# Averages of three heads by column groups in quarters, spread by transfers, with DVE's slots laid out anew and layer one's weight sums on POOL

## The chip, the cores and the metric

One core of a Trainium2 chip runs the whole program. The engines are PE (TensorE, matrix products), DVE (VectorE), ACT (ScalarE), POOL (GpSimd) and SP (SyncE, which here issues most transfers). The metric is the device time of one execution in microseconds (us); lower is better.

## The reference, cut to what matters

The program is one inference step of a two-layer decoder. Layer one (layer A) has an mLSTM branch with four heads of 256 channels and an attention branch over a memory; layer two (layer B) attends over windows. A prompt of 1024 tokens and eight single samples go through it together, so W = 1032 columns (1024 + 8) stand side by side. The change touches the end of the mLSTM branch:

```
(C1, n1, m1), hs = lax.scan(_mlstm_chunk_step, ...)
h = sigmoid(o_pre) * hs                          # per head, 256 channels
mu = mean(h, axis=-1)                            # over the head's 256 channels
var = mean(square(h - mu), axis=-1)
hn = (h - mu) * rsqrt(var + EPS) * g_hn
y = hn + skip * xc
y_mix = y * silu(zg)
```

Here `o_pre`, `zg` and others come from the product `z = rmsnorm(x) @ w_in_a`, which runs while the heads are finished.

## The kernel before

Channels lie on partitions and tokens in columns: a head is two tiles of 128 x 1032 (`big(6 * h)` and `big(6 * h + 1)`), and two more (`HELD[h]`) are its scratch.

**Products.** All projections are made by a scheme with seven smaller products in the place of eight (Strassen's, Winograd's form). A *slot* is one such product: four f32 matmuls of 128 x 258 on PE (L3206, eight records in the trace, since each f32 matmul makes two). A *unit* is seven slots, and two units share one *pair* of weight tiles, so a pair lasts 14 slots. In layer A the loop variable x counts the slots, 0 to 153. Slot x runs product j = x % 7 of its unit. DVE adds five of the seven products into the unit's tiles, a slot later and from PSUM: U2 after j = 1 (L3392), U3 after j = 3 (L3394), C22 (L3397), C21 (L3400) and C12 (L3403). PE waits for them: j = 3 for U2, j = 0 for the previous unit's U3, j = 1 for its C21, j = 4 for its C12, j = 6 for C22. U2 and C22 are the tight ones: the sum can start when slot 1 (5) of the unit ends, and PE wants it one slot later, at the start of slot 3 (6).

**Weights.** SP loads a pair of weight tiles (1 MB, `RING<-in_w_in_a`) at the start of each 14 slots. The scheme wants sums of the tiles. In layer A, DVE makes them in slots 10 and 11 of each 14 (`sum_pair_dve`, L2800 to L2809, five instructions of up to 128 x 512); in layer B, POOL does (`sum_pair`, L2780 to L2788, in instructions of 128 x 256, 384 and 128).

**Heads.** `GATE = (7, 35, 63, 91)` says at which slot x each head begins; n = x - GATE[h]. DVE (`head_dve`, L1484 on): n = 0, 1 small sample operations (L1476 to L1479) and the gates (L1494, two of 128 x 1032); n = 6 the sum of the head's two tiles (L1497, "values sum"); n = 10, 11 centre (L1502, minus the mean, which it reads in PSUM); n = 14 the sum of the squares (L1507); n = 20, 21 norm (L1512); n = 22, 24 skip (L1519); n = 25, 27 the multiplication with zg (L1528; for head 3 at slots 129 and 131). The averages over a head's channels are PE's: `average` (L1341) multiplies the summed tile with a 128 x 128 matrix of 1/256, so each row of the result holds the same averages for all columns. They stand at MEAN = GATE + 8 and VAR = GATE + 16, behind the first matmul of that slot. ACT squares (GATE + 12), takes the logarithm from PSUM (`root_log`, GATE + 17) and the exponential (`root_exp`, GATE + 18) into `ROOT`, a 128 x 1032 tile. SP loads the skip tiles `xc` of heads 2 and 3 at GATE of two heads before + 26.

**State pairs.** The samples' 32 states (8 samples, 4 heads) are updated one after the other by `states_at`, at x % 7 = 2 and 5: SP loads, POOL multiplies (L1200, two of 128 x 256), ACT reduces and decays (L1215, L1208), DVE adds (L1230, two), SP stores. Two buffers take turns, XTRA and TRIG (every fourth is TRIG). The last of them is made near slot 86.

Each engine runs its instructions in the order in which the program writes them, and waits on semaphores. Nothing is moved by a scheduler: a stalled instruction holds all behind it on its engine.

## Time and profile before

| what | us |
| --- | --- |
| median of 3 runs | 1780.26 |
| lowest and highest | 1778.36 and 1782.37 |
| the profiled execution | 1782.37 |
| its span, first to last instruction | 1780.5 |

The profiled execution is the slowest of the three, 2.1 us above the median; 1.9 us of it lie outside the span. The profile has for each engine its busy time, groups of instructions with their mean duration, a chain of waits followed back from the end, and rows in order of time. In these a row joins a few like instructions, "[idle before <-releaser]" tells how long the engine had stood and who let it go on, and a PE row is longer than its slot by the matmul's tail, so that slots are read from the starts. PE is a matmul, PEld the load of its weights.

### The profile page before, as it was taken

Reading aid. Unit: us, or ns where it says so; the run is one execution under the profiler, and the core shown is the slowest. Engines: PE = TensorE matmul, PEld = TensorE weight load, DVE = VectorE, ACT = ScalarE, POOL = GpSimd, SP = SyncE. Lnnn points to the kernel's source line nnn. Section 1 sums busy time; section 2 is a strip of 40 time slices with the busy share of each in tenths; the row PEclk is TensorE's granted clock in tenths of the full one; section 3 lists DMA queues with packets and bytes.
Section 4 is the critical chain, followed back from the end, with each engine's and each line's share of the span. In section 5 each row is a group of like instructions: output and inputs, shape, how many; then the busy total and the mean of one; then the engine's idle time right before and its main releaser. Section 6 shows DMA issues by size and latency. Waiting matters only on the chain.

```text
span 1780.5 us, 22514 instructions
## 1 busy us (share of the span) xinstructions
PE 1754.5 (99%) x8318; PEld 1377.2 (77%) x8318; DVE 855.3 (48%) x1799; ACT 617.7 (35%) x1505; POOL 460.6 (26%) x511
## 2 busy tenths in 40 slices
PE   9999999999999999999999999999999999999998
PEld 5577765988888888747558888888888888779573
DVE  1444323785666556451342543354435444776613
ACT  1321234553655245211311133423242334843311
POOL 0151200335222012410003552154326443223000
PEclk9999999999999999999999999999999999999999
DMA  7312112145655245531111112223132434844422
GB/s 267 136 60 68 63 56 60 49 154 170 192 176 162 77 108 156 187 129 48 61 70 48 37 35 91 72 65 107 45 111 72 142 117 127 278 143 148 156 70 96
DMA packets 149078, 196.21 MB, mean 110 GB/s; under 512 B 19083, under 2 KB 108171, under 8 KB 148834
## 3 DMA queue, kind: packets, MB, share of 16 engines
q1 hardware_dynamic: 140708, 174.58, 30.7%
q10 hardware_dynamic: 8262, 20.20, 3.0%
q8 instruction: 66, 1.08, 0.2%
q14 instruction: 42, 0.34, 0.1%
HBM read 156.97 MB, written 37.85 MB: 109 GB/s over the span
## 4 chain that ended last, share of the span: by engine, by line
PE 90%; DVE 5%; ACT 2%; issue 1%; DMA 1%; SPq 0%; POOL 0%; ACTq 0%; DVEq 0%; POOLq 0%
PE PS L3206 49%; PE PS L2241 11%; PE PS L2285 4%; PE PS L2028 3%; PE PS L398 3%; PE PS L572 3%; PE PS L293 2%; PE PS L2064 2%; PE PS L2039 2%; PE PS L2061 1%; PE PS L934 1%; DVE WK L741 1%; PE PS L927 1%; PE PS L1348 1%; PE PS L2253 1%
## 5 line engine op out<-in xcount | busy, mean ns | idle before, releaser
L3206 PE MATMUL PS<-HT,RING 128*128 128x258 f32 (+2 forms) x1776 | 444.4, 382 | 2.7 <-ACT WK L3296 2.2
L3206 PEld LDWEIGHTS PS<-HT,RING 128*128 128x128 f32 x1776 | 329.6, 190 | 48.4 <-ACT WK L3296 3.1
L3296 ACT ACTIVATE BIG<-PS 128x256 f32<-128x256 f32 (+2 forms) x140 | 53.7, 383 | 354.1 <-PE PS L3206 353.6
L3206 PE MATMUL PS<-BIG,RING 128*128 128x258 f32 (+1 forms) x656 | 159.9, 382 | 1.3 <-DVE BIG L3392 1.3
L2241 PE MATMUL PS<-BIG 128*128 128x512 f32 x328 | 147.7, 597 | 0.5 <-DVE BIG L3403 0.5
L3206 PEld LDWEIGHTS PS<-BIG,RING 128*128 128x128 f32 x656 | 123.2, 190 | 19.6 <-DVE BIG L3392 2.1
L2241 PEld LDWEIGHTS PS<-BIG 128*128 128x128 f32 x328 | 60.4, 190 | 69.7 <-issue 68.6
L3206 PE MATMUL PS<-BIG,WK 128*128 128x258 f32 (+1 forms) x448 | 112.4, 382 | 1.0 <-DVE BIG L3392 1.0
L3206 PE MATMUL PS<-HT,CST 128*128 128x256 f32 (+2 forms) x432 | 110.3, 382 | 0.9 <-DVE BIG L3397 0.8
L3206 PEld LDWEIGHTS PS<-BIG,WK 128*128 128x128 f32 x448 | 83.4, 190 | 13.2 <-DVE BIG L3392 1.4
L3206 PEld LDWEIGHTS PS<-HT,CST 128*128 128x128 f32 x432 | 79.6, 190 | 12.5 <-DVE BIG L3397 2.1
L572 PE MATMUL PS<-WK,RING 128*128 128x344 f32 x288 | 84.3, 453 | 0.2 <-ACT BIG L652 0.2
L2080 ACT ACTIVATE WK<-WK 128x128 f32<-128x128 f32 (+1 forms) x96 | 42.4, 443 | 106.0 <-DVE WK L2112 106.0
L3394 DVE TENSOR_TENSOR BIG<-BIG,PS 128x256 f32<-128x256 f32 (+1 forms) x70 | 29.5, 422 | 99.3 <-PE PS L3206 99.2
L572 PEld LDWEIGHTS PS<-WK,RING 128*128 128x128 f32 x288 | 54.7, 190 | 28.7 <-ACT BIG L652 0.8
L2750 ACT ACTIVATE RING<-RING,VEC 128x256 f32<-128x256 f32 x176 | 74.7, 497 | 2.1 <-DMA RING<-in_w_kv_b 1.1
L3206 PE MATMUL PS<-WK,RING 128*128 128x256 f32 x288 | 73.5, 381 | 0.1
L3413 DVE TENSOR_TENSOR BIG<-BIG,TRIG 64x1024 f32<-64x1024 f32 (+1 forms) x48 | 67.6, 1408 | 1.2
L3067 POOL TENSOR_TENSOR BIG<-BIG 128x512 f32<-128x512 f32 x48 | 60.9, 1280 | 6.1 <-DVE BIG L3422 6.1
L3392 DVE TENSOR_TENSOR BIG<-BIG,PS 128x256 f32<-128x256 f32 (+1 forms) x70 | 29.5, 422 | 65.9 <-PE PS L3206 65.2
L3206 PEld LDWEIGHTS PS<-WK,RING 128*128 128x128 f32 x288 | 52.8, 191 | 7.1 <-DVE BIG L3392 0.7
L3400 DVE TENSOR_TENSOR BIG<-BIG,PS 128x256 f32<-128x256 f32 (+1 forms) x70 | 29.6, 423 | 57.8 <-PE PS L3206 57.6
(402 smaller groups left out, 3155.0 us busy)
## 6 DMA issues: line engine op xcount, KB each, us to landing
RING<-in_w_in_a SPq DMA_DIRECT2D x14, 1024.0 KB, 6.0
WK<-in_cache_mem_kv SPq DMA_DIRECT2D x56, 256.0 KB, 5.7
RING<-in_w_kv_b SPq DMA_DIRECT2D x12, 1024.0 KB, 5.6
RING<-in_w_in_b SPq DMA_DIRECT2D x12, 1024.0 KB, 5.3
WK<-in_cache_win SPq DMA_DIRECT2D x40, 256.0 KB, 4.6
RING<-in_w_mkv SPq DMA_DIRECT2D x16, 512.0 KB, 4.6
BIG<-in_x_prompt SPq DMA_DIRECT2D x16, 512.0 KB, 3.2
BIG<-sample_query SPq DMA_DIRECT2D x28, 256.0 KB, 5.8
```

Source lines behind the costliest of these rows:

```text
L293: last = nc.tensor.matmul(PS[:, s + b, 0:SEG], w[:, kt * P:(kt + 1) * P], rhs(kt, b * SEG, (b + 1) * SEG), start=(kt == 0), stop=(kt == kt ...
L398: last = nc.tensor.matmul(PS[:, 4 + 2 * nt + half, :], MEMT[:, kt, nt * P:(nt + 1) * P], w[:, half * 512:(half + 1) * 512], start=(kt == 0 ...
L572: last = nc.tensor.matmul(PS[:, s + b, 0:SEG], w[:, c:c + P], rhs, start=(kt == 0), stop=(kt == 1))
L2028: last = nc.tensor.matmul(bank[:, x * nk:(x + 1) * nk], q, k, start=True, stop=True)
L2080: last = nc.scalar.activation(p, PS[:, 3 + u % 2, x * nk:(x + 1) * nk] if g in MEM else p, ACT.Exp, bias=negmax[:, x:x + 1], scale=1.0 if ...
L2241: last = nc.tensor.matmul(PS[:, BANKS[i] + half, :], c.src(kt, u * P, (u + 1) * P), c.piece(kt)[:, half * 512:(half + 1) * 512], start=(kt ...
L2285: last = nc.tensor.matmul(PS[:, 6 + n % 2, 0:COLS], c.piece(kt)[:, n * P:(n + 1) * P], c.src(kt, 6 * P, W), start=(kt == 0), stop=(kt == c ...
L2750: last = nc.scalar.activation(x, x, ACT.Copy, scale=VEC[:, k, row:row + 1])
L3067: last = nc.gpsimd.tensor_tensor(perm(dst, d)[:, j0:j1], natural(big(RAW + x, 0, T), d)[:, j0:j1], natural(big(TURN + x, 0, T), d)[:, j0:j ...
L3206: last = nc.tensor.matmul(PS[:, bank, 0:mid - lo], weight_block(u // 2, s, k), h_block(layer_of(u), u % 2, t, k), start=(k == 0 and j not ...
L3296: nc.scalar.activation(part(u, n2 if j == 0 else n1, lo, mid), PS[:, banks(u)[0], 0:mid - lo], ACT.Copy).then_inc(sig("projections_copied" ...
L3413: last = nc.vector.tensor_tensor(y[q:q + 64], x[p:p + 64], TRIG[p:p + 64, W + lo:W + hi] .rearrange("p (t n) -> p t n", t=1).to_broadcast( ...
```

## The change

**Averages.** For heads 0 to 2 (`SPREAD = 3`) an average is four matmuls, each with 32 of the matrix's columns and a quarter of the tokens (258). They go to four groups of 32 rows in one PSUM bank, so that row group g holds quarter g. The mean stands at GATE + 4, the variance still at GATE + 16. Head 3 keeps the old form.

**Spread.** ACT brings the strip of 128 x 258 to `ROOT` (`mean_strip` at MEAN + 1, or logarithm at VAR + 1 and exponential at VAR + 2), and saves four rows of it, one of each group, to DRAM (`save_average`). At MEAN + 3 and VAR + 4 it waits for that and issues a transfer that reads the 1032 numbers back to all 128 rows of `ROOT` (`spread_average`, 516 KB written). DVE's centre and norm wait for it and read `ROOT`.

**DVE's slots for heads 0 to 2.** Gates 0, 1; values sum 3 (6 before); centre 10, 11; squares 14; norm 24, 25 (20, 21); skip 27, 32 (22, 24); zg 34, 35 (25, 27). For head 3: zg at 38, 40, as before; nothing else differs. Since the next head's gates stand at n = 28 and 29, norm, skip and zg of a head now surround these. The `xc` loads of heads 2 and 3 move from + 26 to + 33.

**Weight sums.** `sum_pair_dve` is gone; `sum_parts` on POOL makes layer A's sums too, in three parts at x % 14 = 5 (four instructions), 8 (two) and 9 (two), each behind what POOL has queued before.

```diff
-            job(f"mean{h}", "dve")
+            job(f"mean{h}", "act" if h < SPREAD else "dve")
...
-        MEAN = [x + 8 for x in GATE]
+        MEAN = [x + (4 if h < SPREAD else 8) for h, x in enumerate(GATE)]
         VAR = [x + 16 for x in GATE]
+        QUARTER = W // 4
...
-                    if x == GATE[h - 2] + 26:
+                    if x == GATE[h - 2] + 33:
...
         def layer_a_pool(pool):
+            parts = iter(())
             for x in range(XA):
                 for i in states_at(x + 2):
                     pair_pool(pool, i)
+                p = PF + x // 14 + 1
+                if x % 14 == 5 and p < PA:
+                    parts = sum_parts(pool, p)
+                if x % 14 in (5, 8, 9):
+                    next(parts, None)
...
-            for b in range(3):
-                last = nc.tensor.matmul(AVERAGED[:, b, :], avg_h, big(HELD[h][0], b * SEG, (b + 1) * SEG),
-                                        start=True, stop=True)
+            if h < SPREAD:
+                for g in range(4):
+                    last = nc.tensor.matmul(PS[32 * g:32 * (g + 1), 3, 0:QUARTER], avg_h[:, 0:32],
+                                            big(HELD[h][0], g * QUARTER, (g + 1) * QUARTER), start=True, stop=True)
...
+            act.dma_start(avg_rows_d[2 * h + var].rearrange("(g n) -> g n", g=4),
+                          ROOT[0:P:32, 0:QUARTER]).then_inc(average_saved(h, var)[0], 16)
...
+            act.wait_ge(*average_saved(h, var))
+            act.dma_start(ROOT, avg_rows_d[2 * h + var].partition_broadcast(P)).then_inc(average_spread(h, var)[0], 16)
...
+            nc.scalar.activation(ROOT[:, 0:QUARTER], PS[:, 3, 0:QUARTER], ACT.Copy).then_inc(job_read["act"].up(), 1)
+            save_average(act, h, 0)
...
+                        if x == MEAN[h] + 1:
+                            mean_strip(act, h)
+                        if x == MEAN[h] + 3:
+                            spread_average(act, h, 0)
+                        if x == VAR[h] + 4:
+                            spread_average(act, h, 1)
...
-            if n == 6:
+            if n == (3 if h < SPREAD else 6):
...
+            norm, skip, gated_at = ((24, 25), (27, 32), (34, 35)) if h < SPREAD else ((20, 21), (22, 24), (38, 40))
...
+                if h < SPREAD:
+                    dve.wait_ge(*average_spread(h, 0))
+                    ins = nc.vector.tensor_tensor(y, y, ROOT, ALU.subtract)
...
+                dve.wait_ge(*(average_spread(h, 1) if h < SPREAD else (sig("root_ready").sem, h + 2)))
...
-                if PF + x // 14 + 1 < PA and x % 14 in (10, 11):
-                    for n in ((0, 1), (2, 3))[x % 14 - 10]:
-                        sum_pair_dve(dve, PF + x // 14 + 1, n)
```

The order of instructions shows it. PE, head 0's mean in slots 14 and 15, before (a product is "x4" there):

```order
L3206 MATMUL PS<-HT,CST 128x258 x4
L3206 MATMUL PS<-HT,RING 128x258 x4
L3206 MATMUL PS<-BIG,WK 128x258
L1348 MATMUL PS<-BIG,CST 128x344 x3
L3206 MATMUL PS<-BIG,WK 128x258 x3
```

and after, in slots 11 and 12:

```order
L3252 MATMUL PS<-BIG,RING 128x258 x4
L3252 MATMUL PS<-HT,RING 128x258
L1358 MATMUL PS<-BIG,CST 32x258 x4
L3252 MATMUL PS<-HT,RING 128x258 x3
L3252 MATMUL PS<-BIG,RING 128x258 x4
```

The average is four matmuls of 32 x 258 where it was three of 128 x 344, and four slots earlier.

DVE, slots 62 to 67, where head 2's gates stand (L1230 is a state pair, TRIG or XTRA its buffer), before:

```order
L3400 TENSOR_TENSOR BIG<-BIG,PS 128x258
L1528 TENSOR_TENSOR BIG<-BIG 128x1032
L3403 TENSOR_TENSOR BIG<-BIG,PS 128x258
L1476 TENSOR_TENSOR SM<-SM 128x16
L1477 TENSOR_TENSOR SM<-SM 128x16
L1479 TENSOR_TENSOR BIG<-SM 128x2x8
L1494 TENSOR_TENSOR BIG<-BIG 128x1032 x2
L3392 TENSOR_TENSOR BIG<-BIG,PS 128x258
L1230 SCALAR_TENSOR_TENSOR XTRA<-XTRA,SM 128x256 x2
L2800 TENSOR_TENSOR WK<-RING 128x512
L2804 TENSOR_TENSOR RING<-RING 128x4x128
L3394 TENSOR_TENSOR BIG<-BIG,PS 128x258
```

and after:

```order
L3446 TENSOR_TENSOR BIG<-BIG,PS 128x258
L1581 SCALAR_TENSOR_TENSOR BIG<-WK,VEC,BIG 128x1032
L3449 TENSOR_TENSOR BIG<-BIG,PS 128x258
L1530 TENSOR_TENSOR SM<-SM 128x16
L1531 TENSOR_TENSOR SM<-SM 128x16
L1533 TENSOR_TENSOR BIG<-SM 128x2x8
L1548 TENSOR_TENSOR BIG<-BIG 128x1032 x2
L3438 TENSOR_TENSOR BIG<-BIG,PS 128x258
L1232 SCALAR_TENSOR_TENSOR XTRA<-XTRA,SM 128x256 x2
L1551 TENSOR_TENSOR BIG<-BIG 128x1032
L3440 TENSOR_TENSOR BIG<-BIG,PS 128x258
```

Head 1's skip (L1581) stands where its zg (L1528) stood, and head 2's values sum (L1551) where two of the weight sums stood.

POOL has state products and nothing else through layer A before (L1200). After, at the same stretch, it has:

```order
L1202 TENSOR_TENSOR WK<-TRIG 128x256 x2
L2845 TENSOR_TENSOR WK<-RING 128x256 x2
L2847 TENSOR_TENSOR RING<-RING 128x2x128 x2
L1202 TENSOR_TENSOR WK<-XTRA 128x256 x2
L2851 TENSOR_TENSOR WK<-RING 128x256 x2
L2854 TENSOR_TENSOR WK<-RING,WK 128x384
L2855 TENSOR_TENSOR WK<-RING,WK 128x128
L1202 TENSOR_TENSOR WK<-XTRA 128x256 x4
```

Eight weight sums stand among eight state products of 14 slots.

## Rows read from the trace of the kernel before

**Rows 1.** The page: busy times of the engines, granted clock of PE, chain of waits.

```profile
PE 1754.5 (99%) x8318; PEld 1377.2 (77%) x8318; DVE 855.3 (48%) x1799; ACT 617.7 (35%) x1505; POOL 460.6 (26%) x511
...
PEclk9999999999999999999999999999999999999999
...
PE 90%; DVE 5%; ACT 2%; issue 1%; DMA 1%; SPq 0%; POOL 0%; ACTq 0%; DVEq 0%; POOLq 0%
```

**Rows 2.** The averages' line: durations in ns (min/median/max), first and last start.

```profile
L1348 PE MATMUL PS<-BIG,CST x48: 452/453/453, 445.8 to 619.7; 128*128 128x344 f32 x48
```

**Rows 3.** PE's timeline at head 0's mean: start, us, engine, line, operation.

```profile
443.67 1.90 PE L3206 MATMUL PS<-HT,RING 128*128 128x258 f32 x8
445.41 0.60 PE L3206 MATMUL PS<-BIG,WK 128*128 128x258 f32 x2
445.84 1.90 PE L1348 MATMUL PS<-BIG,CST 128*128 128x344 f32 x6
447.58 1.47 PE L3206 MATMUL PS<-BIG,WK 128*128 128x258 f32 x6
448.88 1.90 PE L3206 MATMUL PS<-HT,RING 128*128 128x258 f32 x8
```

**Rows 4.** PE's timeline at the 32-column matmuls of L584.

```profile
259.68 3.93 PE L572 MATMUL PS<-WK,RING 128*128 128x344 f32 x13
263.54 10.62 PE L584 MATMUL PS<-BIG,TRIG 128*32 128x344 f32 x144
274.09 2.00 PE L293 MATMUL PS<-HT,RING 128*128 128x344 f32 x6
276.02 1.93 PE L594 MATMUL PS<-WK,TRIG 128*36 128x344 f32 x6
277.88 2.29 PE L293 MATMUL PS<-HT,RING 128*128 128x344 f32 x7
```

**Rows 5.** The weight loads of L584, timeline of PEld.

```profile
273.11 0.13 PEld L584 LDWEIGHTS PS<-BIG,TRIG 128*32 128x32 f32 x4 [0.16 <-issue]
273.40 0.13 PEld L584 LDWEIGHTS PS<-BIG,TRIG 128*32 128x32 f32 x4 [0.16 <-issue]
```

**Rows 6.** Timeline of DVE and POOL side by side, after layer A.

```profile
740.58 2.39 POOL L2780 TENSOR_TENSOR RING<-RING 128x256 f32<-128x256 f32 x2 [3.08 <-PE PS L3206]
...
740.81 6.57 DVE L2007 TENSOR_TENSOR BIG<-BIG 128x1024 f32<-128x1024 f32 x4
...
742.93 3.37 POOL L2782 TENSOR_TENSOR RING<-RING 128x256 f32<-128x256 f32 x2
```

**Rows 7.** Timeline of DVE and PE around head 2's gates.

```profile
536.48 0.36 DVE L1476 TENSOR_TENSOR SM<-SM 128x16 f32<-128x16 f32 x1
...
537.25 2.50 DVE L1494 TENSOR_TENSOR BIG<-BIG 128x1032 f32<-128x1032 f32 x2
...
539.67 0.42 DVE L3392 TENSOR_TENSOR BIG<-BIG,PS 128x258 f32<-128x258 f32 x1
540.00 0.88 DVE L1230 SCALAR_TENSOR_TENSOR XTRA<-XTRA,SM 128x256 f32<-128x256 f32 x2
...
541.16 1.91 PE L3206 MATMUL PS<-BIG,RING 128*128 128x258 f32 x8
```

**Rows 8.** POOL's state products: ns min/median/max.

```profile
L1200 POOL TENSOR_TENSOR WK<-XTRA x36: 722/740/1838, 421.5 to 569.0; 128x256 f32<-128x256 f32 x36
```

**Rows 9.** Transfers: size, median us to landing, issued from 321, 523 and 743.

```profile
WK<-mlstm_rows SPq DMA_DIRECT2D x1, 512.0 KB, 3.8
...
RING<-in_w_in_a SPq DMA_DIRECT2D x1, 1024.0 KB, 6.5
...
WK<-in_g_post ACTq DMA_DIRECT2D x1, 512.0 KB, 12.4
```

**Rows 10.** Timeline of POOL and DVE at head 0's TRIG state.

```profile
454.01 1.41 POOL L1200 TENSOR_TENSOR WK<-TRIG 128x256 f32<-128x256 f32 x2 [14.85 <-DMA TRIG<-sample_q_and_weighted_k]
...
457.42 0.41 DVE L3400 TENSOR_TENSOR BIG<-BIG,PS 128x258 f32<-128x258 f32 x1
```

More of the change, by code:

```diff
@@ L1346, in average, with average_saved, average_spread, save_average @@
                 pe.wait_ge(*read_of(f"mean{h}" if name[0] == "v" else f"var{h - 1}"))
-            for b in range(3):
-                last = nc.tensor.matmul(AVERAGED[:, b, :], avg_h, big(HELD[h][0], b * SEG, (b + 1) * SEG),
-                                        start=True, stop=True)
-            last.then_inc(job_done.up(), 1)
+            if h < SPREAD:
+                for g in range(4):
+                    last = nc.tensor.matmul(PS[32 * g:32 * (g + 1), 3, 0:QUARTER], avg_h[:, 0:32],
+                                            big(HELD[h][0], g * QUARTER, (g + 1) * QUARTER), start=True, stop=True)
+            else:
+                for b in range(3):
+                    last = nc.tensor.matmul(AVERAGED[:, b, :], avg_h, big(HELD[h][0], b * SEG, (b + 1) * SEG),
+                                            start=True, stop=True)
+            last.then_inc(job_done.up(), 1)
+        def average_saved(h, var):
+            return sig("scratch_saved").sem, 80 + 16 * (2 * h + var + 1)
+        def average_spread(h, var):
+            return sig("rows0_broadcast").sem, 16 * 3 + 16 * (2 * h + var + 1)
+        def save_average(act, h, var):
+            act.wait_ge(*(sig("root_ready").sem, h + 2) if var else read_of(f"mean{h}"))
+            act.dma_start(avg_rows_d[2 * h + var].rearrange("(g n) -> g n", g=4),
+                          ROOT[0:P:32, 0:QUARTER]).then_inc(average_saved(h, var)[0], 16)
+        def spread_average(act, h, var):
+            act.wait_ge(*average_saved(h, var))
+            act.dma_start(ROOT, avg_rows_d[2 * h + var].partition_broadcast(P)).then_inc(average_spread(h, var)[0], 16)
+        def mean_strip(act, h):
+            act.wait_ge(job_done.sem, done(f"mean{h}"))
+            if h > 0:
+                act.wait_ge(sig("y_ready").sem, 2 * h - 1)
+            nc.scalar.activation(ROOT[:, 0:QUARTER], PS[:, 3, 0:QUARTER], ACT.Copy).then_inc(job_read["act"].up(), 1)
+            save_average(act, h, 0)
         def woven_a_pe(pe, x):
@@ L1412, in root_log @@
             act.wait_ge(job_done.sem, done(f"var{h}"))
-            if h > 0:
+            if h < SPREAD:
+                nc.scalar.activation(ROOT[:, 0:QUARTER], PS[:, 3, 0:QUARTER], ACT.Ln,
+                                     bias=EPSC).then_inc(job_read["act"].up(), 1)
+            else:
                 act.wait_ge(sig("y_ready").sem, 2 * h - 1)
-            nc.scalar.activation(seg3(ROOT), AVERAGED, ACT.Ln, bias=EPSC).then_inc(job_read["act"].up(), 1)
+                nc.scalar.activation(seg3(ROOT), AVERAGED, ACT.Ln, bias=EPSC).then_inc(job_read["act"].up(), 1)
         def root_exp(act, h):
             act.wait_ge(*read_of(f"var{h}"))
-            nc.scalar.activation(ROOT, ROOT, ACT.Exp, scale=-0.5).then_inc(sig("root_ready").up(), 1)
+            root = ROOT[:, 0:QUARTER] if h < SPREAD else ROOT
+            nc.scalar.activation(root, root, ACT.Exp, scale=-0.5).then_inc(sig("root_ready").up(), 1)
+            if h < SPREAD:
+                save_average(act, h, 1)
         def gate_act(act, u):
@@ L1498, in head_dve @@
                                         ALU.add).then_inc(sig("values_summed").up(), 1)
[L1499 to L1502 removed]
+            centre, summed = 10, 14
+            norm, skip, gated_at = ((24, 25), (27, 32), (34, 35)) if h < SPREAD else ((20, 21), (22, 24), (38, 40))
+            if n in (centre, centre + 1):
+                e = n - centre
+                y = big(6 * h + e)
+                if h < SPREAD:
+                    dve.wait_ge(*average_spread(h, 0))
+                    ins = nc.vector.tensor_tensor(y, y, ROOT, ALU.subtract)
+                else:
+                    dve.wait_ge(job_done.sem, done(f"mean{h}"))
+                    ins = nc.vector.tensor_tensor(seg3(y), seg3(y), AVERAGED, ALU.subtract)
                 if e == 1:
[L1504 to L1505 removed]
+                    ins.then_inc((sig("values_summed") if h < SPREAD else job_read["dve"]).up(), 1)
+            if n == summed:
                 dve.wait_ge(sig("squares").sem, h + 1)
@@ L1508, in head_dve @@
                                         ALU.add).then_inc(sig("squares_summed").up(), 1)
-            if n in (20, 21):
-                y, j = big(6 * h + n - 20), 2 * h + n - 20
-                dve.wait_ge(sig("root_ready").sem, h + 2)
+            if n in norm:
+                e = norm.index(n)
+                y, j = big(6 * h + e), 2 * h + e
+                dve.wait_ge(*(average_spread(h, 1) if h < SPREAD else (sig("root_ready").sem, h + 2)))
                 nc.vector.scalar_tensor_tensor(out=y, in0=y, scalar=vec(ROW_GHN, j), in1=ROOT,
                                                op0=ALU.mult, op1=ALU.mult).then_inc(step.up(), 1)
-            if n in (22, 24):
-                e = (n - 22) // 2
+            if n in skip:
+                e = skip.index(n)
                 y, j = big(6 * h + e), 2 * h + e
@@ L2759, in sum_pair, with sum_parts @@
         def sum_pair(pool, p):
+            for _ in sum_parts(pool, p):
+                pass
+        def sum_parts(pool, p):
+            if p == PF + 1:
+                pool.wait_ge(sig("h_turned").sem, NU)
             if p < PA:
@@ L2783, in sum_pair @@
             then(last, 5)
+            yield
             for k in parts:
```

46 lines of the change are left out of this document (12 added, 34 removed).

## The prediction, before the kernel was run

> **What bounds the kernel now.** I read the page first. PE is busy for 99% of the span, at a granted clock of nine tenths or more in all forty slices, and the chain of waits that ended last lies for 90% on PE and for 5% on DVE [rows 1]. So what PE issues is the time, as long as nobody makes it wait. The reader should then look at the stretch where the averages stand. Their source line shows 48 matmul records of 453 ns, two per matmul, 24 matmuls in 8 averages [rows 2]. The PE timeline has no wait in brackets there, and shows that an average pushes the rest of its slot aside: the records of L1348 begin at 445.84 and the product goes on at 447.58, 1.74 us later; a slot without an average takes 443.67 to 445.41, also 1.74 us [rows 3]. One average is therefore worth a whole slot of PE, all of it on the path. In slots 0 to 111 every slot is 1.74 us but the eight with an average, at 3.47: PE waits for nobody there before the change, so each new wait shows in full.
>
> **What PE saves.** Six of the eight averages become four matmuls of 32 columns in four column groups. The trace has this form in L584: 144 matmuls of 32 columns, 344 wide [rows 4]; their weight loads come in fours, the fours 0.29 us apart (273.11 to 273.40) [rows 5]. That is the time of one full pass of 344 columns: the six records of L1348 take 1.74 us, 0.29 each [rows 3]. Four column groups thus share one pass. The new form is 258 wide; a slot has 8 passes of that width in 1.74 us, 0.217 each, and every f32 matmul makes two: 2 x 0.217 = 0.43 us. Going into that form and back costs something. In [rows 4] the 13 passes of L572 before it should end at 259.68 + 13 x 0.289 = 263.44 and L584 starts at 263.54 (0.11); its 36 passes should end at 273.94 and L293 starts at 274.09 (0.15). The 36-column form of L594 is dearer: 274.09 + 6 x 0.289 = 275.82 against 276.02 (0.20), and 276.02 + 6 x 0.289 = 277.75 against 277.88 (0.13). I take the dearer, 0.33, as the excursion is as short as that one. An average then costs 0.43 + 0.33 = 0.77 and saves 1.74 - 0.77 = 0.97; six save **5.8 us**. The bounds are 5.4 (switch 0.4) and 7.8 (no switch cost).
> The Trainium skill ("TensorE: Matmul & The Clock Gate", Measured speedup vs the span model) gives 2.38 times for three column tiles, 79% of the ideal; by it each pass of four would be 0.275 us and the six averages 0.7 us dearer, an estimate from that page, while L584 shows the whole factor.
>
> **What is moved beside PE.** ACT now copies or roots 258 columns instead of 1032, shorter than before. It adds two issues per average, on ACT's own queue; ACT is busy 35% of the span and delays nobody by them. DVE loses in ten weight pairs the five sums of L2800 to L2809, and POOL gets them: eight instructions for each pair. The last pairs' slots (121, 135) have waits for ACT and DVE today; the sums' going gives back perhaps 0.2 there, and as much may be lost, so nothing is entered. DVE's centre operations read SBUF instead of PSUM, for the same 1.2 us.
>
> **What POOL's sums cost DVE.** The trace shows what happens when POOL adds in SBUF while DVE runs operations with two SBUF operands. From 740.81 four DVE operations on 1024 columns take 6.57 us, 1.64 each, while POOL's take 1.19 and 1.69 [rows 6]; a lone DVE operation of 1032 takes 1.25 (2.50 for two) [rows 7], and a lone POOL one 0.72, with a maximum of 1.84 [rows 8]. DVE loses about 0.44 us for every POOL instruction that falls beside such work. Sums that read PSUM are never stretched (0.42 everywhere).
> The place where this matters is where a head's gates stand, since the two large multiplications are just ahead of a sum that PE needs. Head 2: before, smalls from 536.48, gates from 537.25, then the U2 sum, which ends at 540.09; PE takes its result at 541.16 [rows 7]. Slack 1.07. After, POOL has work all through it. The pair's load is issued at 523.9, lands after 6.5 us [rows 9], say at 531 with the spread beside it, and behind it stand eight sums and at least four state products at 1 to 1.2 us each: to about 543. The three smalls meet it (0.2 each is my estimate, between 0 and 0.4), and the two gates (0.44 each): 0.6 + 0.88 = 1.5. The work ahead (second norm from about 531, a pair of state operations, skip) is met by 1.2 more, of which I let only 0.1 pass: before the smalls stands a product sum that comes no earlier whatever DVE does. The U2 sum ends at 540.09 + 1.5 + 0.1 = 541.7, 0.5 after PE wants it.
> What is late next: the values sum now stands three slots behind the gates, after a pair of state operations (0.79) [rows 7]. From 541.65: 0.79 + 0.87 for two meetings, then 1.23 + 0.44, end 545.0. The average of slot 67 wants it one matmul into its slot: 541.16 + 1.74 = 542.9 [rows 7], + 0.5 + 0.43 = 543.8. PE waits another 1.15. **Head 2's window gives back 1.65.** Bounds: 0, if half of the meetings fall elsewhere, and 3.3 with twice the meetings.
> Head 1's window is built alike, with its norm a little later since its spread is: **1.8**. Head 3's has no state products left and its load lands earlier in it, and its values sum stays six slots behind the gates: 0 to 0.3, I take **0.1**.
>
> **The transfers.** Each new average is saved (4 rows of 258) and read back as a broadcast of 516 KB. The nearest rows are 3.8 us for a broadcast of 512 KB alone, 6.5 for 1 MB while others run, and 12.4 us for one of 512 KB issued by ACT into loaded queues [rows 9]. I take 4 to 5.5: around head 1 to 3 the queues carry one weight pair and small state loads. The mean's spread has two us to spare. The variance's is issued 0.8 us ahead of slot 56 (up to 2 us after slot 28), and DVE's norm can take it up to 6.6 us after its issue before the sums behind it are late. Nothing is entered; the upper end is a rival.
> Head 0 has another chain at that place. SP's loads into TRIG are released by the head's work; now PE's average stands four slots earlier, so what was loaded in slot 22's run-up comes 0.77 later against PE, and slot 22 starts 0.97 earlier. Before, POOL waits for that load at 454.01, and the C21 sum behind the TRIG pair ends at 457.83; slot 22 wants it at 448.88 + 6 x 1.74 = 459.3 [rows 3, 10]. Slack 1.5 less 1.74 leaves -0.24, and the spread shares the engines: **0.35** (0 to 1.5).
>
> **Sum.** Saved 5.8; given back 1.65 + 1.8 + 0.1 + 0.35 = 3.9. Net 1.9. The profiled execution has 1782.37 us, 2.1 above the median; so 1780.5 for a profiled run like it, and 1780.3 - 1.9 = **1778.4** against the median.
>
> **Rivals.**
> *The meetings are absorbed.* POOL's sums start early, or DVE's operations are stretched by less where POOL's are spaced by its waits; PE never waits. For it: the windows have 1.07 us of slack and the state products of POOL are spaced today (median 0.74, hardly stretched) [rows 8]. Against it: twelve or more instructions in a row and DVE busy from 531 on. Then 1780.3 - 5.8 + 0.35 = 1774.8; without a switch cost 1772.8.
> *The spreads land late: slower.* One mechanism: the 516 KB broadcast shares sixteen engines with the weight pair that SP issues within 2 us of it, and takes as long as the loaded one of [rows 9]. It decides from 6.6 us after the issue: DVE stands at the norm, and the sums of products queue behind it, and PE behind them. At 9 us the wait is 2.4 us for each of three heads: 7.2 more, 1785.5. Against it: 1 MB lands in 6.5 us in this very place.
> *DVE pays a whole POOL instruction.* Were each meeting to cost DVE all of POOL's 0.72 instead of 0.44, then some ten meetings in two windows cost 0.28 more each, some 2.2 a window on both: 1782.8. The row speaks against it (1.64, not 1.96) [rows 6].
> The Trainium skill ("SBUF — State Buffer", SBUF: two separate sides) states just this: an exclusive lock for the whole instruction between GpSimd and a DVE operation with two SBUF inputs, "the other fully blocks". The contention the trace agrees with, its full size not.
> *The column groups don't run side by side.* Eight passes of 0.217 and 0.33: 2.07 for an average against 1.74, 2 us lost where 5.8 should be won, and the windows' loss on top: 1786. L584's fours speak against it.
>
> **How the numbers follow.** Forecast 0.46; absorbed 0.34; late spreads 0.12; whole blocking 0.05; no packing 0.03. The measurement tells 0.2%, 3.6 us, from no change: below 1776.7 is faster, above 1783.8 slower. Faster takes the absorbed case and a tail of the forecast less a tail of the absorbed: 0.36. Slower takes the late spreads and no packing, less a little: 0.14. Same: 0.50. The range goes from the absorbed case with half the switch cost, 1773.8, to just short of the late spreads, 1784.0. The forecast's own range is 1775.5 to 1781.
>
> **What the new profile would show.** L1358's averages with 0.7 to 0.8 us between the product records around them; if 1.7, the packing fell. DVE's gates at 1.3 to 1.7 instead of 1.25 in heads 1 and 2, with PE idle in the slots that follow (three and four slots behind the gates' slot), released by DVE; if PE has no such idle time, my collisions were too dear and the time is near 1775. DVE idle before the norm or centre, released by a DMA into ROOT, would speak for the late spreads. The forecast fails most easily on the size and place of the meetings, as POOL's queue is ordered by waits and not by slots.

## The result: slower, and where the profile shows it

The changed kernel takes 1789.82 us (median of 6 runs, 1788.1 to 1793.12) against 1780.99 for the kernel before in the same comparison: a ratio of 1.0048, 95% interval 1.0038 to 1.0057. That is 8.8 us more, where the prediction had 1.9 less. The second rival of the prediction, spreads that land late, is what happened, and it cost more than the rival was given.

The page of the changed kernel, the lines that answer to [rows 1]:

```profile
span 1788.7 us, 22585 instructions
...
PE 1753.2 (98%) x8330; PEld 1369.5 (77%) x8330; DVE 836.9 (47%) x1749; ACT 615.6 (34%) x1508; POOL 533.7 (30%) x591
...
PE   9999999999899999999999999999999999999998
...
PE 81%; DVE 6%; issue 4%; ACT 4%; POOL 2%; DMA 2%; SPq 0%; ACTq 0%; DVEq 0%; POOLq 0%
```

PE is busy 1.3 us less and the span is 8.2 us longer: PE now waits. POOL has 73 us more work. PE's share of the chain of waits falls by 9 points, which go to issue, ACT, POOL, DVE and DMA. One slice of PE's row in layer A shows an 8 (the very last slice had its 8 before the change too).

The saving is there, as forecast. L1358, the average's line now (answers to [rows 2]), and the PE timeline at head 0's mean (answers to [rows 3]):

```profile
L1358 PE MATMUL PS<-BIG,CST x48: 381/393/406, 436.0 to 575.3; 128*32 128x258 f32 x48
```

```profile
435.48 0.60 PE L3252 MATMUL PS<-HT,RING 128*128 128x258 f32 x2
436.00 0.64 PE L1358 MATMUL PS<-BIG,CST 128*32 128x258 f32 x8
436.58 1.57 PE L3252 MATMUL PS<-HT,RING 128*128 128x258 f32 x6
437.99 1.91 PE L3252 MATMUL PS<-BIG,RING 128*128 128x258 f32 x8
```

That slot lasts 437.99 - 435.48 = 2.51 us where one without an average lasts 1.74: 0.77 for an average that cost 1.73.

The rest is in what PE waited for. In layer A's stretch (415 to 610) the kernel before has one wait of PE on the view, 1.6 us, ahead of the products. The changed kernel has these (engine, line, releaser: us in all, times, longest), and below them DVE's waits for the spreads, at the centre (L1560) and at the norm (L1574):

```profile
PE PS L3252 <- DVE BIG L3443: 8.6, 3, 3.9
PE PS L1358 <- DVE BIG L1551: 1.3, 2, 0.7
PE PS L3252 <- DVE BIG L3446: 0.9, 1, 0.9
PE PS L3252 <- DVE BIG L3438: 0.8, 1, 0.8
```

```profile
DVE BIG L1560 <- DMA WK<-head_averages: 9.3, 2, 5.4
...
DVE BIG L1574 <- DMA WK<-head_averages: 7.8, 2, 5.8
```

The largest sits in slot 33. The timeline of DVE there, then of PE:

```profile
471.79 0.87 DVE L1232 SCALAR_TENSOR_TENSOR XTRA<-XTRA,SM 128x256 f32<-128x256 f32 x2
478.50 1.67 DVE L1574 SCALAR_TENSOR_TENSOR BIG<-BIG,VEC,WK 128x1032 f32<-128x1032 f32 x1 [5.84 <-DMA WK<-head_averages]
480.09 0.41 DVE L3440 TENSOR_TENSOR BIG<-BIG,PS 128x258 f32<-128x258 f32 x1
480.43 1.42 DVE L1574 SCALAR_TENSOR_TENSOR BIG<-BIG,VEC,WK 128x1032 f32<-128x1032 f32 x1
481.77 0.41 DVE L3443 TENSOR_TENSOR BIG<-BIG,PS 128x258 f32<-128x258 f32 x1
```

```profile
476.47 1.91 PE L3252 MATMUL PS<-BIG,RING 128*128 128x258 f32 x8
482.23 3.55 PE L3252 MATMUL PS<-HT,CST 128*128 128x258 f32 x8 [3.86 <-DVE BIG L3443]
485.57 2.09 PE L3252 MATMUL PS<-HT,RING 128*128 128x258 f32 x8
```

DVE stands 5.84 us at the norm, since head 0's variance is not back. Two sums of products queue behind the two norms, and PE stands behind the second sum. When PE goes on, its slot takes 3.34 us, not 1.74. The same stretch by windows (us, PE busy, granted clock, share of the transfer engines, GB/s) says why:

```profile
470.00:476.50 6.50, 6.50 (x32) 1.00 0.85 278
476.50:482.20 5.70, 1.88 (x9) 1.00 0.34 121
482.20:485.60 3.40, 3.37 (x9) 0.55 0.32 89
485.60:489.00 3.40, 3.40 (x16) 0.95 0.41 143
```

After 3.86 us of PE's idleness the granted clock falls to 0.55, about the 1.2 GHz level, for 3.4 us, and then comes back to 2.4 GHz.

Slot by slot (from the starts of PE's products), slots 0 to 111 of layer A take 209.81 us before and 221.16 after, 11.35 more:

| slots | what | us |
| --- | --- | --- |
| 11, 15, 23, 39, 43, 51, 67, 71, 79 | six averages (slots 15, 43 and 71 lose their average, 11, 39 and 67 get it) | -5.78 |
| 33 to 35 | variance of head 0 late, the clock's fall 1.8 of it | +5.81 |
| 47, 48 | mean of head 1 late | +2.04 |
| 75 to 77 | mean of head 2 late, the clock's fall 1.8 of it | +4.89 |
| 21, 22 | head 0's TRIG state | +1.14 |
| 37 to 39 | head 1's gates and values sum | +1.08 |
| 65 to 67 | head 2's gates and values sum | +1.78 |
| 93, 94 | head 3's gates | +0.40 |

So the spreads' own slots cost 12.7 us, and the places that the prediction had priced cost 4.4 where it had 3.9.

The profiled execution reached slot 0 3.0 us earlier than the one before, in work that the change doesn't touch; hence 8.2 in the span and 11.4 in layer A. The timed runs put the change at 8.8.

### The profile page after: what moved, and what is told of

Same layout as the page of the kernel before. It is cut to its first block, busy times and chain, and to the rows that moved or that the text cites. A ratio compares the mean times of both kernels' runs of the same rounds, so it can differ in the third digit from the quotient of the medians.

```text
span 1788.7 us, 22585 instructions
## 1 busy us (share of the span) xinstructions
PE 1753.2 (98%) x8330; PEld 1369.5 (77%) x8330; DVE 836.9 (47%) x1749; ACT 615.6 (34%) x1508; POOL 533.7 (30%) x591
## 4 chain that ended last, share of the span: by engine, by line
PE 81%; DVE 6%; issue 4%; ACT 4%; POOL 2%; DMA 2%; SPq 0%; ACTq 0%; DVEq 0%; POOLq 0%
PE PS L3252 42%; PE PS L2299 11%; PE PS L2343 4%; PE PS L400 3%; PE PS L2086 3%; PE PS L574 3%; PE PS L295 2%; PE PS L2122 2%; PE PS L2097 2%; PE PS L2119 1%; DVE WK L743 1%; PE PS L936 1%; DMA WK<-head_averages 1%; PE PS L929 1%; POOL WK L1202 1%
## 5 line engine op out<-in xcount | busy, mean ns | idle before, releaser
L574 PEld LDWEIGHTS PS<-WK,RING 128*128 128x128 f32 x288 | 54.6, 190 | 28.7 <-ACT BIG L654 0.6
L3440 DVE TENSOR_TENSOR BIG<-BIG,PS 128x256 f32<-128x256 f32 (+1 forms) x70 | 29.5, 421 | 93.1 <-PE PS L3252 93.1
L2847 POOL TENSOR_TENSOR RING<-RING 128x256 f32<-128x256 f32 x76 | 68.8, 926 | 0.0
L2845 POOL TENSOR_TENSOR WK<-RING 128x256 f32<-128x256 f32 x34 | 28.1, 849 | 130.5 <-ACT RING L2808 86.1
L2845 POOL TENSOR_TENSOR RING<-RING 128x256 f32<-128x256 f32 x36 | 29.9, 852 | 100.9 <-ACT RING L2808 66.2
```

Of the source, the lines that this page charges most:

```text
L574: last = nc.tensor.matmul(PS[:, s + b, 0:SEG], w[:, c:c + P], rhs, start=(kt == 0), stop=(kt == 1))
L2845: nc.gpsimd.tensor_tensor(s3[:, k], a11[:, k], a21[:, k], ALU.subtract)
L2847: last = nc.gpsimd.tensor_tensor(a21[:, k], a21[:, k], a22[:, k], ALU.add)
```

## Why the spreads were late

When each spread (516 KB) was issued and landed, beside the weight pair (1 MB) of its time:

| spread | issued | pair issued | spread took |
| --- | --- | --- | --- |
| mean 0 | 438.84 | 442.28 | 4.0 |
| variance 0 | 469.71 | 468.16 | 8.8 |
| mean 1 | 500.90 | 500.00 | 7.7 |
| variance 1 | 527.37 | 527.19 | 6.5 |
| mean 2 | 555.13 | 554.28 | 9.0 |
| variance 2 | 583.39 | 584.17 | 4.5 |

The two that are issued ahead of their pair land in 4.0 and 4.5 us, the four behind it in 6.5 to 9.0. The packets say it directly. Of mean 1's spread (issued at 500.90 on ACT's queue, q10), in the view of transfers from 501 to 503.8, and then from 503.8 to 508.6:

```profile
q1 hardware_dynamic: 681, 0.79, 93.9%
q10 hardware_dynamic: 1, 0.00, 2.0%
```

```profile
q1 hardware_dynamic: 948, 0.95, 65.2%
q10 hardware_dynamic: 143, 0.52, 33.3%
```

For almost 3 us SP's queue moved 0.79 MB and ACT's next to nothing; then the spread went through. Not all of this is the pair's doing. The two spreads that are issued ahead also need 1.0 us before their first row moves; the four behind a pair need 2.6 to 4.1. And SP's queue held two state loads of 256 KB as well, issued 2.7 and 2.2 us ahead of mean 1's spread. The Trainium skill ("DMA: Bandwidth & Descriptors", Queues, rings and completion order) says that each engine takes turns between the queues that have work, packet by packet. Here the later queue's transfer did not get its turns at once: until a tenth of a late spread's rows had moved, SP's queue had moved 0.6 to 1.1 MB in the four cases. The measurement decides for this kernel.

The spread is only the second of two transfers in a row. The save of 4 KB ahead of it stands behind other loads in the same way: it took 1.6 to 2.4 us for mean 0 and the three variances, but 4.4 for mean 1 and 3.4 for mean 2. These two are issued 0.5 and 1.6 us behind the two `xc` loads of 516 KB, which the change itself had moved into slots 40 and 68:

```profile
496.00 0.81 SPq L1283 DMA_DIRECT2D WK<-xc_scratch  x2
496.49 0.50 ACTq L1377 DMA_DIRECT2D head_averages<-WK  x1
```

A mean has less time than a variance: DVE stood at head 1's centre from 504.7, 8.2 us after that save was issued.

## The experiments

Layer A means slots 0 to 111 of the profiled execution, against 209.81 us; the ratio is that of timed runs to the kernel before on the same chip, with its 95% interval.

**The spread ahead of the pair.**

```diff
+                if x % 14 == 0 and x // 14 in (2, 3, 4, 5):
+                    spread_average(sp, (x // 14 - 1) // 2, (x // 14 - 1) % 2)
                 if x % 14 == 0 and p >= PF + 2:
                     load_pair(sp, p)
...
-                        if x == MEAN[h] + 3:
+                        if x == MEAN[h] + 3 and h == 0:
...
-                        if x == VAR[h] + 4:
+                        if x == VAR[h] + 4 and h == 2:
```

> The changed kernel, but the four spreads that stood behind a weight pair in the transfer engines (variance of heads 0 and 1, mean of heads 1 and 2) are issued by SP just ahead of that pair. Theory 'queue': a spread is late because its packets stand behind the pair's 1 MB; in the changed kernel it landed in 4.0 and 4.5 us when issued ahead and 6.5 to 9.0 us when issued behind. It then expects four landings of 4 to 5 us and the long slots 33, 34, 47, 48, 75 and 76 back at 1.74 us, 12.5 us less: about 1777.5. Rival 'bytes': the 516 KB share the engines with the pair whichever comes first, landings stay at 7 to 9 us, and the time stays within 2 us of 1790. Rival 'POOL': the long slots come mostly from POOL's sums beside DVE; landings fall but less than half of the 12.5 us comes back: about 1784.

Layer A +0.36 us, ratio 1.0001 (0.9991 to 1.0010). The spreads' line:

```profile
L1385 SPq DMA_DIRECT2D WK<-head_averages x4: 332/332/332, 471.6 to 551.0; - x4
...
DMA to landing us min/median/max: 4.1/5.3/6.4
```

It was 4.0/7.1/9.0. Slots 33 to 35 are 1.74 again, 47 and 48 have 0.42 left and 75 and 76 0.48: 11.8 of 12.7 us came back. The edit changes two things, the order and the queue (SP's for ACT's). That the order counts with the queue kept shows in the spreads that ACT issues, in all kernels here: 15 issued ahead of the pair of their time landed in 3.9 to 4.8 us, 18 behind it in 5.6 to 9.0. Variance 2, which is always ACT's, lies on both sides: 4.5 to 4.8 ahead (5 times), 5.6 to 6.3 behind (6 times). Issued by SP ahead of the pair they took 4.6 to 7.0, so what else is under way costs something there too (6.4 for mean 1 here). Theory 'queue' holds; a rival 'bytes', with landings of 7 to 9 us, does not.

In the timed runs 8.4 us came back by the two ratios, some 4 less than I had expected. Of these, 0.9 is what slots 47, 48, 75 and 76 keep, and 0.8 is new: slots 37 to 39 lose 2.14 for 1.08 and head 3 0.57 for 0.40, while 65 to 67 (1.51) and 21 and 22 (1.02) lose a little less than before. The rest is that the profiled execution of the changed kernel showed more than its timed runs, 11.4 against 8.8. It may be that one wait had covered others: while PE was held up in slots 33 to 35, POOL's queue went on and met less of what came behind. No run shows this by itself, but the second execution of the changed kernel, further below, fits it: 6.7 us lost in slots 33 to 35 and nothing in 37 to 39.

**No spread.** The two issues are left out, and DVE's waits go to the save.

> The changed kernel without its spreads: the averages are saved, but not read back to all rows, so centre and norm use what lies in the tile. DVE waits for the save alone. Theory 'queue' and theory 'bytes' expect the same: slots 33, 34, 47, 48, 75 and 76 at 1.74 us, 12.5 us less, about 1777; the windows after the gates (slots 37 to 39 and 65 to 67) keep their 1.3 and 1.8 us, and head 0's slot 21 keeps about 1 us. Rival 'POOL' expects long slots there still, 1784 or more.

Layer A -3.67, ratio 0.9979 (0.9970 to 0.9989). All six slots are at 1.74. Left are 0.32 (slots 21, 22), 0.93 (37 to 39) and 0.87 (65 to 67). The timed runs say the same. So in this order of DVE's and POOL's work the change wins 3.7 without any spread, not 5.8. Against this run the changed kernel's profile has 15.0 us more, of which 12.7 are the spreads' own slots; the other 2.3 lie in slots 21, 22, 37 to 39, 65 to 67, 93 and 94, and whether the spreads' traffic makes them is not shown. The rival 'POOL' is out: no long slot is left.

**POOL's sums alone.**

```diff
 # the kernel before, and
+                if x % 14 == 5 and p < PA:
+                    parts = sum_parts(pool, p)
+                if x % 14 in (5, 8, 9):
+                    next(parts, None)
...
-                if PF + x // 14 + 1 < PA and x % 14 in (10, 11):
-                    for n in ((0, 1), (2, 3))[x % 14 - 10]:
-                        sum_pair_dve(dve, PF + x // 14 + 1, n)
```

> The kernel before, with one part of the change alone: layer one's weight sums on POOL in the same three parts. Averages, transfers and DVE's slots as before. By my sum the meetings of POOL's sums with DVE cost about 1.5 us in each of the two windows after the gates of heads 1 and 2; the values sum stands six slots behind the gates here and so waits for nobody. Expected: 0.5 to 1 us in slot 37 and in slot 65, nothing in slots 39 and 67, about 1782. Rival 'POOL': the sums cost several us, 1786 or more. Rival 'free': no slot gets longer, 1780 to 1781.

Layer A +1.71, ratio 1.0007 (0.9998 to 1.0017). Slots 37 and 38 lose 0.76, 65 and 66 lose 0.96, all others nothing. DVE and POOL around head 2's gates in this kernel:

```profile
536.91 0.59 DVE L1485 TENSOR_TENSOR BIG<-SM 128x16 f32<-128x16 f32 x1
537.61 3.58 DVE L1500 TENSOR_TENSOR BIG<-BIG 128x1032 f32<-128x1032 f32 x2
541.12 0.41 DVE L3383 TENSOR_TENSOR BIG<-BIG,PS 128x258 f32<-128x258 f32 x1
```

```profile
536.72 1.45 POOL L2796 TENSOR_TENSOR WK<-RING 128x256 f32<-128x256 f32 x2
538.24 1.86 POOL L2799 TENSOR_TENSOR WK<-RING,WK 128x384 f32<-128x384 f32 x1
540.07 1.44 POOL L2800 TENSOR_TENSOR WK<-RING,WK 128x128 f32<-128x128 f32 x1
```

The two gates take 3.58 us where they took 2.50 [rows 7]: 1.64 for the one that meets one POOL instruction and 1.91 for the one that meets two, 0.40 and 0.34 for each, where the prediction had 0.44. Even the operation on 16 columns takes 0.59 where it took 0.17.

**POOL's later parts held until the values sum**, for each head's gates.

```diff
-                if x % 14 in (5, 8, 9):
+                held_by = x // 28 if x // 14 in (0, 2, 4, 6) else None
+                if x % 14 in (5, 10, 11) if held_by is not None else x % 14 in (5, 8, 9):
+                    if held_by is not None and x % 14 == 10:
+                        pool.wait_ge(sig("values_summed").sem, 2 * held_by + 1)
                     next(parts, None)
```

> As the kernel with the spreads first, and in the 14 slots of each head's gates POOL's second and third part (four instructions) wait for the head's values sum, so that they don't meet the gates. Theory: the windows of slots 37 to 39 and 65 to 67 give back 1.3 and 1.8 us by meetings; half of those are with the held parts. Expected 1.0 to 2.5 us less than with the spreads first: about 1776. Rival: the state products alone meet the gates as often, and nothing changes beyond 0.5 us; or the sums come too late for slot 1 of the next pair and PE waits there.

Layer A +5.46, ratio 1.0032 (1.0021 to 1.0042). A miss, by one place: head 3's values sum stands six slots behind its gates, so its parts came too late, and PE stood 5.1 us on L2860, POOL's last sum, with the clock's fall behind it (7.8 us in slots 97 to 99). Elsewhere it lost 2.7 us less than with the spread first, a little more than expected.

**The same for three heads** (`(0, 2, 4)`).

> As e4_sums_held, without the holding in head 3's slots, whose values sum stands six slots behind its gates. Theory: the 7.8 us that slots 97 to 99 lost in e4_sums_held came from that holding alone and go; head 3's slot 93 has its 0.4 us back. Against the kernel before: saved 5.8, given back 0.2 (slot 21), 1.7 (37 to 39), 1.1 (65 to 67), 0.4 (93), 0.2 (117): 2.2 us faster than before, about 1779.5 on this chip. Rival: the held sums are late in other pairs too once these stalls are gone, and it is at the time of before.

Layer A -1.61, ratio 0.9994 (0.9984 to 1.0005), which the timed runs can't tell from no change. The 7.8 us are gone; slot 37 lost 1.58 where the same code had lost 0.50 in the run before: what meets what differs from one execution to the next.

**The values sum ahead of the state pair, and then the second gate behind the U2 sum.**

```diff
+                for h in range(H):
+                    if x == GATE[h] + 2:
+                        head_gate_dve(dve, h, 1)      # only in the second kernel
+                        if h < SPREAD:
+                            values_sum_dve(dve, h)
                 for i in states_at(x):
                     pair_dve(dve, i)
```

> As e5_held_three_heads, with the values sum of heads 0 to 2 ahead of the state pair that stands behind the gates. Theory: the average in slot 39 waits for the pair in front of the values sum (1.7 to 2.1 us with its meetings and its wait for ACT). Without it slot 39 loses its 1.1 us of wait; slots 37 and 65 keep 0.5 and 1.0, since the U2 sum stands ahead of both. 1.1 us faster than e5_held_three_heads. Rival: the pair, now later, makes PE or the next state late, and the gain is under 0.3 us.

> As e6_values_sum_ahead, with the second gate of each head behind the U2 sum, which the first gate alone then stands ahead of. Theory: PE's waits in slots 37, 65 and 93 come from the U2 sum behind two stretched gates (1.65 us each); with one of them moved, they go: 0.5, 1.0 and 0.4 with 0.1 each for going on, 2.0 us less than e6_values_sum_ahead. The values sum is 0.4 us later and its average in slots 39 and 67 may wait up to 0.5 us. About 1776. Rival: the sum of the three operations is the limit and PE's wait moves whole to slots 39 and 67, no gain.

Layer A +1.06 and +2.89, ratios 0.9999 (0.9990 to 1.0009) and 1.0009 (0.9999 to 1.0018). In each the aimed-at wait went: slots 39 and 67 have no wait in the first, slots 37, 65 and 93 none in the second. Yet in the profiled executions both lost more in layer A than the kernel that they started from (-1.61); the timed intervals overlap, so the runs leave this open. Most of what was new is in slots 47, 48 and 75 to 77, which lost 2.6 and 5.7 us: the means' spreads went out late, in slots 43 and 71, then in 44 and 72 (42 and 70 in the kernel that they started from). I took SP's store of the later state pair for the cause, since it stands ahead of the spread in SP's queue, and the next experiment was built on that. The trace says otherwise. What SP waited for at mean 1's spread (L1388) in the second kernel is the save (SP's waits from 490 to 500):

```profile
SPq L1388 <- DMA head_averages<-WK: 2.1, 1, 2.1
```

The two means' saves took 5.4 and 6.1 us in the first kernel and 5.8 and 6.8 in the second, where they had taken 4.2 and 4.5; all of them are issued 0.5 us behind the two `xc` loads. Why they are slower here is not shown. Neither my theory nor the rival had this.

**The mean's spread on ACT again, and then the TRIG state's loads ahead of the pair of slot 14.**

```diff
-                if x % 14 == 0 and x // 14 in (2, 3, 4, 5):
+                if x % 14 == 0 and x // 14 in (2, 4):
...
+                if x == GATE[0] + 7:                  # only in the second kernel
+                    pair_load(sp, EARLY_STATES + 3)
                 if x % 14 == 0 and p >= PF + 2:
                     load_pair(sp, p)
...
-                        if x == MEAN[h] + 3 and h == 0:
+                        if x == MEAN[h] + 3:
```

> As e7_second_gate_later, but the means' spreads are issued by ACT again; SP still issues the variance's of heads 0 and 1 ahead of its pair. Theory: in e7_second_gate_later SP came to the mean's spread only in slots 44 and 72, since the state pair behind the values sum is later and SP's store of it stands ahead; so DVE's centre was late and slots 47, 48 and 75 to 77 lost 5.7 us. ACT can issue them at slot 42 and 70 + 1 us: 4 to 5 us less than e7_second_gate_later, about 1778. Rival: ACT's spread then shares with SP's two state loads and lands after 6 us or more; half of the loss stays.

> As e9_mean_by_act, and at slot 14 SP issues the loads of the TRIG state ahead of the weight pair instead of behind it. Theory: slot 21's wait (0.8 to 1.4 us in the kernels with spreads) is the TRIG state landing behind the pair's 1 MB at slot 20; ahead of it, it lands before slot 18 and the wait goes: 1 us less than e9_mean_by_act, 3 us less than the kernel before. Rival: slot 21 waits for something else, POOL's or ACT's work on that state, and the gain is under 0.3 us; or the pair, now behind, makes POOL's sums late.

Layer A +6.51 and +1.26, ratios 1.0026 (1.0014 to 1.0038) and 1.0010 (1.0001 to 1.0019). The first is a miss, since its theory had the wrong cause. ACT has to wait for the save just as SP had:

```profile
493.99 0.48 ACTq L1382 DMA_DIRECT2D head_averages<-WK  x1
499.73 0.34 ACTq L1388 DMA_DIRECT2D WK<-head_averages  x1
500.17 0.39 ACT L3358 ACTIVATE BIG<-PS 128x258 f32<-128x258 f32 x1 [4.74 <-DMA head_averages<-WK]
```

So ACT issued the spreads 2.3 and 1.5 us into slots 43 and 71, 2.2 and 2.1 us behind SP's pair, and they landed after 6.6 and 6.5 us, in slots 47 and 75. ACT's copies of products stood behind that wait too, and PE waited 1.3 and 0.5 us for them in slots 43 and 71.

The second removes slot 21's wait whole (1.35 us to 0), as expected, though this kernel too is not faster than the kernel before. How long before slot 22's turn the TRIG loads land goes with the loss in slots 21 and 22 in every kernel here: 5.4 us in the kernel before and 7.1 in this one, no loss; 4.4, 0.08 lost; 4.3, 0.23; 3.4, 1.14; 3.0, 1.46.

**The changed kernel again.**

> The changed kernel once more, for its stalls from execution to execution. Theory: each spread behind a pair lands late in each execution; slots 33, 47 and 75 are long again by 1.5 us or more each, 8 to 13 us in sum, and the clock falls only behind those waits that are over about 2 us. Rival: the profile first seen was one of the bad ones, and the sum here is under 8 us. The part ahead of layer A, which the change does not touch, should differ by up to 3 us either way.

Layer A +8.70, ratio 1.0044 (1.0028 to 1.0059). The spreads behind their pair took 8.1, 7.9, 6.8 and 7.5 us, those ahead 4.2 and 4.5. Slots 33 to 35 lost 6.7, 47 and 48 1.1, 61 and 62 1.2, 75 and 76 2.5: 11.6 in all. The smaller losses are not stable: slots 21 and 22 lost 0.08 (1.14 in the first execution), 37 to 39 nothing (1.08), 65 to 67 2.08 (1.78), 93 and 94 0.67 (0.40). Again it reached slot 0 3.4 us earlier than the kernel before. What I expected of the clock ("over about 2 us") is too simple: the granted clock fell to half, the 1.2 GHz level, behind PE waits of 3.6 us here and of 2.1 us (twice) in the kernel with the mean on ACT, but stayed at 1.00 behind one of 2.3 us here.

**The first order of DVE's work, spreads and TRIG ahead**: the kernel for three heads with the TRIG loads moved.

> As e5_held_three_heads (both gates, U2 sum, state pair, values sum; all four shared spreads by SP ahead of its pair), and at slot 14 the TRIG state's loads ahead of the weight pair. Theory: e5_held_three_heads lost in layer A 0.9 us in slots 21 and 22, 2.4 in 33 to 38, 0.8 in 65 and 66, 0.5 in 93 and 94; the first goes as in e10_trig_ahead, and the mean's spreads don't come late as in the two kernels with the state pair moved. In layer A 2 to 2.5 us less than the kernel before. Rival: with slot 21's wait gone SP or DVE is late in another place and it is at the time of before.

Layer A -4.67, ratio **0.9978** (0.9969 to 0.9987): 1777.08 us against 1780.92, and by the two ratios some 12.5 us below the changed kernel. Of the 5.8 us saved it gives back 1.1: 0.20 in slots 37 and 38, 0.40 in 65 and 66, 0.40 in 93 and 94. It beats both kernels, by more than I expected: slots 33 to 38, which had lost 2.0 us, lost 0.2. No run tells how much of that is the moved load and how much is from execution to execution. Slots 0 to 36 have no wait at all.

**Variances alone, DVE keeps its sums.** The kernel before; only `var0` to `var2` in column groups, spread by SP in slots 28 and 56 and by ACT in 83; norm, skip and zg at 24, 25, 27, 33, 35, 36.

> The kernel before with one part of the change in a smaller form: only the variances' averages of heads 0 to 2 are in column groups and spread (by SP ahead of its pair for heads 0 and 1); means as before, DVE keeps the weight sums in its slots 10 and 11, POOL has state products alone, norm, skip and the zg multiplication are later (24, 25, 27, 33, 35, 36). Theory: three slots (23, 51, 79) are 0.97 us shorter, 2.9 us, and nothing is given back since no sum of POOL meets a gate and each spread has its landing to spare: layer A 2.9 us shorter, about 0.16%. Rival: without POOL's help DVE's slots 11 and 12 with two weight sums and a skip make PE wait 1 us for each of two heads, and at least 1.5 us is given back.

Layer A -2.90, ratio 0.9985 (0.9977 to 0.9994). Slots 23, 51 and 79 are 0.965 us shorter each, 2.90 in sum, and no other slot in 0 to 111 differs by 0.03 us. This shows both the size of the saving and that the column groups and a spread that lands in time cost nothing by themselves. What the changed kernel loses therefore comes with the rest of the change: the mean's earlier time, the order and company of the transfers, and POOL's sums.

## The prediction, step by step

- **What bounds the kernel**: right. PE has no wait in slots 0 to 111 before the change, so each new wait shows whole. (Slot 1 is a ninth slot that is not 1.74 long: 2.62, before and after.)
- **What PE saves**: right, 0.77 for an average (forecast 0.77), 5.78 in all (5.8). The dearer switch cost was the right choice. The figure of the Trainium skill ("TensorE: Matmul & The Clock Gate", Measured speedup vs the span model), 2.38 times for three tiles, would have made it 0.7 us less; the trace does not agree with it for four.
- **What POOL's sums cost DVE**: right in mechanism and, for head 2 in this execution, nearly in size. Head 2's window lost 1.78 (forecast 1.65): 0.97 and 0.10 at the U2 sum, 0.71 at the values sum. The rows that answer to [rows 7]:

```profile
541.66 3.33 DVE L1548 TENSOR_TENSOR BIG<-BIG 128x1032 f32<-128x1032 f32 x2
544.91 0.41 DVE L3438 TENSOR_TENSOR BIG<-BIG,PS 128x258 f32<-128x258 f32 x1
```

```profile
545.38 2.01 PE L3252 MATMUL PS<-BIG,RING 128*128 128x258 f32 x8 [0.80 <-DVE BIG L3438]
547.22 0.60 PE L3252 MATMUL PS<-HT,RING 128*128 128x258 f32 x2
548.46 0.64 PE L1358 MATMUL PS<-BIG,CST 128*32 128x258 f32 x8 [0.64 <-DVE BIG L1551]
```

  The gates meet POOL once each, 1.65 instead of 1.25. Head 1's window lost 1.08 (forecast 1.8) in the changed kernel, nothing in its second execution, and 2.14 once the spread was on time. Head 3's was 0.40, not 0.1. That the three terms together came out near the forecast (3.3 for 3.55) is in part luck: head 1's alone runs from 0 to 2.1 over these executions.
- **Head 0's TRIG chain**: right in mechanism, mis-sized: 1.14 for 0.35. Against slot 22 the loads landed 2.0 us nearer (forecast 1.74), and DVE's two operations on that state took 1.74 us beside POOL's sums of the next pair, where they had taken 1.29: 1.5 - 2.0 - 0.45 is 1.0 short, and 0.1 for going on. I had not entered POOL's new sums in this chain. In the second execution the loads came only 1.0 us nearer and 0.08 was lost.
- **The transfers: the step that failed.** "I take 4 to 5.5 ... Nothing is entered." The spreads behind a pair took 6.5 to 9.0 us and cost 12.7. The rows for a better estimate were in [rows 9]: 512 KB take 3.8 and 1 MB takes 6.5, so 512 KB more cost about 2.7, and a spread that stands behind 1 MB would land after about 9.2, the upper end of what was measured. I had listed the pair as light company, when in four of six cases it was issued 0.2 to 1.6 us ahead of the spread, on the same engines. I also wrote that the mean's spread has two us to spare. But mean 1 was issued a microsecond behind the pair, in slot 42, and DVE wanted it at 504.7, only 3.8 us later, less than any spread took. And the save ahead of the spread had no term at all: it took 4.4 and 3.4 us for means 1 and 2, not 1.7, behind the `xc` loads that the change had moved there.
- **The second rival** had the sign and the mechanism of the shared engines right, and put 0.12 on it. It had the place right for one of three: it spoke of the norms of three heads with 6.6 us of room. Head 0's norm was late (8.8 us); head 1's variance landed after 6.5 us and cost nothing, as the 6.6 says, and head 2's was ahead of its pair. The other two late ones were the centres of heads 1 and 2. Its price of 2.4 us for each head was near 2.04, but short of 5.81 and 4.89: it lacked the clock's fall (1.8 us, twice) and the norms or centres and sums that queue behind the wait.
- **Whole blocking**: no. A gate that meets POOL takes 1.65, as the row that I chose said: DVE loses 0.41, not 0.72. It is POOL that loses more, 1.71 for an instruction of 0.73. The rival's price was also added up wrongly: ten meetings at 0.28 are 2.8 us, 1781.2, and not 4.4 and 1782.8.
- **The range**: 1784.0 "just short of the late spreads" was cut where the rival began.

## What to carry to other kernels

A transfer that is waited for should be issued ahead of the large ones of its time, whatever queue it is on. Price it as the bytes in front of it and its own, look up what else is issued within 2 us, and do so for each link of a chain: here a save of 4 KB, issued just behind 1 MB, took 4.0 to 6.8 us. A step that frees PE makes the deadlines behind it earlier by as much, and each place where the slack is 1 us is then to be worked out anew with its new company. When an issue comes late, look up what it waited for before moving it to another engine.

## What the runs showed of the hardware

- A transfer on ACT's queue issued 0.9 us behind 1 MB of SP's: its first row moved after 2.6 us, and one packet in the first 2.8, where a transfer issued ahead of such a load starts after 1.0 us. A save of 4 KB issued 0.5 us behind two loads of 516 KB took 4.0 to 6.8 us; the saves without such loads took 1.6 to 2.9.
- A wait of PE costs 0.10 us more than itself: the slot that follows takes 1.85, also where slot 37 was only 0.09 longer (slots 37 and 38 of the fastest kernel). A row of it in the changed kernel is that at 545.38, 2.01 long instead of 1.91.
- After waits of 2.9 and 3.9 us the granted clock was 0.56 and 0.55, about the 1.2 GHz level, for some 3.4 us, which costs another 1.8 us; after one of 1.8 us it stayed at 1.00. In the second execution it was 0.51 for 6.8 us behind a wait of 3.6, which cost about 3.
- DVE loses 0.3 to 0.5 us for each POOL instruction that it meets with operands in SBUF, also in an operation of 0.17 us; POOL's own of 0.73 takes 1.7 beside a gate.
- What stays open: both profiled executions of the changed kernel reached slot 0 3.0 and 3.4 us before the kernel before did, though the code ahead is the same; the others lay between 2.1 us earlier and 2.2 later. No run here tells whether that is chance.
